# Expert biases as rows of a row group, loaded per block, with the first expert blocks and the record placing rearranged

## The chip, the cores and the metric

The kernel runs on one core of a Trainium2 chip. The metric is the device time in microseconds of one execution, as the median of repeated runs. The engines are PE (TensorE), DVE (VectorE), ACT (ScalarE), POOL (GpSimd) and SP (SyncE, which here only issues transfers).

## What is computed

A decoder block over 512 tokens of width 1024: a token mixer (gated short convolution and dilated attention), then a mixture of 32 experts, of which each token takes 4. The change touches the second part:

```python
logits = (hf @ w_router + b_router).astype(jnp.float32)
top_vals, top_idx = lax.top_k(logits, TOP_K)
gates = jax.nn.softmax(top_vals, axis=-1)
...
def expert_block(args):          # xb: 128 rows of one expert e
    xb, e = args
    gu = xb @ w_gate_up[e] + b_gate_up[e]
    gate, up = gu[:, :D_EXPERT], gu[:, D_EXPERT:]
    gate = jnp.minimum(gate, SWIGLU_LIMIT)
    up = jnp.clip(up, -SWIGLU_LIMIT, SWIGLU_LIMIT)
    act = (up + 1) * (gate * jax.nn.sigmoid(SWIGLU_ALPHA * gate))
    return act @ w_down[e] + b_down[e]
...
out = jax.ops.segment_sum(y_assign, sorted_tok, num_segments=T)
```

## The kernel before

Every engine's program is written out by hand in its own order; semaphores join them. The front (token mixer) streams 38 chunks of weights of 1 MiB. Its last stage is `wo`, which also gives the router's logits. Then comes **routing**: ranks of the tokens within their experts, the first rows for three experts found early, and `place_records`, which works out for each of the 2048 assignments a slot in a table in DRAM (`slot_dram`).

The **expert part** is a loop over blocks, here 32 (one per expert, 128 rows each). A block's weights are 12 chunks of 1 MiB: c = 0 to 7 are `w_gate_up` of this block's expert, c = 8 to 11 are `w_down` of the block before. For each chunk SP issues the load (`load_expert`, L526) into one of six raw buffers as soon as DVE has read that buffer's last content; ACT writes the upper part of the chunk in fp32r (`split_expert`, L1045), DVE the rest (L1351), into eight half-chunk units. PE multiplies with three products for each pair (`three`, L589): 16 units `gate_up` (L820), then 8 units `down` (L837) of the block before, 144 products of 512 columns in all. `used` counts the units that PE has finished, `split_lo` those that DVE has delivered.

Around these products PE also turns rows. `turn_act` (L805, after j = 1 and j = 3) turns the activations of the block before; `turn_rows` (L799, after k = 1 and k = 3 of `down`, by `next_rows`) the gathered rows of the next block. ACT and DVE copy each turned half out of PSUM (`turned`). POOL gathers rows from DRAM with an indirect transfer, and adds a block's result to `out` with another (`scatter`, with a read and write at the target). The column of indices for both it copies from `slots`, the table read back from DRAM. For blocks 0 to 2 the indices come from the early search instead; the gather of block 2's rows (`gather(4)`) stands on POOL behind the 16 transfers that write the records (L1606).

**Biases.** POOL cuts `b_gate_up` into three bf16 parts, stacked on 96 partitions (L1572 to L1577), and builds `sel`, a 96 x 128 selector for each block (L1579, for blocks past 32 L1641 in `over_step(4)`). In `gate_up` at k = 0 two products of `sel` with 512 columns set the bank (L828), so four a block. `b_down` is not added in the loop. In block 0 DVE makes a token-by-expert matrix of gates (`gates_by_expert`), PE turns it (L866) and multiplies it with `b_down` in fp32, four row groups of 32 for each half of the columns (`down_bias`, L858); ACT stores the result into `x2`, and POOL adds it to `out` by four indirect transfers (L1679) ahead of the loop of scatters.

Before block 0 PE runs `BUSY` = 14 products whose result nobody reads (L812).

## Time and profile before

| | us |
|---|---|
| median of 3 runs (lowest, highest) | 1700.66 (1699.68, 1701.02) |
| the profiled execution | 1699.82 |
| its span, from the first to the last instruction | 1697.8 |
| busy: PE, DVE, ACT, POOL | 1642.9, 1360.8, 1106.0, 330.3 |
| transferred | 484.45 MB, mean 285 GB/s |

The span is 2.0 us shorter than the execution's own time. Starts are given from the span's start. PE's records of successive products overlap (a product of 512 columns is recorded with 0.39 us), so pace is read from start to start, not from the length of a record.

### The profile page before, as it was taken

What the parts mean: (1) busy time and instruction counts of PE and PEld (TensorE: products, weight loads), DVE (VectorE), ACT (ScalarE), POOL (GpSimd) and SP (SyncE); (2) the same over time, 40 slices, a digit from 0 to 9 for tenths busy, and PEclk for the clock granted to TensorE, in tenths of its full rate; (3) what the DMA queues carried; (4) which work ended last, traced back from release to release, by engine and by line L of the source; (5) the groups of instructions that cost most, each with busy time, mean ns of one, the idle gap of its engine ahead of it and who ended that gap; (6) DMA issues with size and microseconds to landing.
All of it is one profiled execution on the core that took longest, in us unless ns stands there. A gap on an engine that the chain in (4) does not pass through costs nothing.

```text
span 1697.8 us, 23948 instructions
## 1 busy us (share of the span) xinstructions
PE 1642.9 (97%) x8021; PEld 1346.8 (79%) x8021; DVE 1360.8 (80%) x1124; ACT 1106.0 (65%) x1004; POOL 330.3 (19%) x176
## 2 busy tenths in 40 slices
PE   8999999999988899999999999999999999999995
PEld 5797777888886778877888888888888888888884
DVE  5974555533558889999999999999998999999994
ACT  5433433422345677877878878788777887777873
POOL 0000000500005523342222211222112211113210
PEclk9999999999998999999999999999999999999998
DMA  7331222332449999999999999999999999999993
GB/s 226 122 100 50 75 75 75 93 116 83 152 179 294 282 384 371 381 379 361 380 375 367 383 376 378 374 366 384 375 378 376 363 382 381 378 375 367 380 383 95
DMA packets 212404, 484.45 MB, mean 285 GB/s; under 512 B 12619, under 2 KB 55283, under 8 KB 195843
## 3 DMA queue, kind: packets, MB, share of 16 engines
q1 hardware_dynamic: 201168, 453.99, 72.4%
q0 software_dynamic: 11200, 29.96, 7.9%
q8 instruction: 25, 0.41, 0.1%
q14 instruction: 11, 0.09, 0.0%
HBM read 469.05 MB, written 23.77 MB: 290 GB/s over the span
## 4 chain that ended last, share of the span: by engine, by line
PE 53%; DVE 0%; issue 0%; ACT 0%; POOL 0%; ACTq 0%; DVEq 0%; POOLq 0%
PE ps L590 17%; PE ps L592 16%; PE ps L591 16%; PE ps L807 1%; PE ps L801 1%; PE ps L828 1%; DVE w_lo L1355 0%; ACT w_hi L1050 0%; POOL out L1667 0%; DVE oT L1512 0%; ACT r L1105 0%; DVE work L1502 0%; ACTq L213 0%; DVEq L1354 0%; ACTq L1049 0%
## 5 line engine op out<-in xcount | busy, mean ns | idle before, releaser
L1355 DVE TENSOR_TENSOR zT<-raw,zT 128x2048 fp32r<-128x2048 f32 x96 | 222.5, 2318 | 53.8 <-ACT zT L1050 51.1
L1355 DVE TENSOR_TENSOR w_lo<-more_raw,w_hi 128x2048 fp32r<-128x2048 f32 x96 | 217.3, 2289 | 24.1 <-ACT w_hi L1050 23.9
L1355 DVE TENSOR_TENSOR zT<-more_raw,zT 128x2048 fp32r<-128x2048 f32 x96 | 220.2, 2293 | 1.1 <-ACT zT L1050 1.1
L1355 DVE TENSOR_TENSOR w_lo<-raw,w_hi 128x2048 fp32r<-128x2048 f32 x96 | 216.7, 2284 | 1.2 <-issue 0.9
L590 PE MATMUL ps<-w_hi,xT 128*128 128x512 f32 x512 | 216.9, 424 | 0.0
L590 PE MATMUL ps<-zT,xT 128*128 128x512 f32 x512 | 203.0, 396 | 0.9 <-DVE zT L1355 0.7
L592 PE MATMUL ps<-w_hi,xT 128*128 128x512 f32 x512 | 201.2, 393 | 0.0
L591 PE MATMUL ps<-w_lo,xT 128*128 128x512 f32 x512 | 200.8, 392 | 0.0
L1050 ACT ACTIVATE zT<-more_raw 128x2048 fp32r<-128x2048 f32 x96 | 183.4, 1911 | 26.0 <-PE ps L592 21.6
L592 PE MATMUL ps<-zT,xT 128*128 128x512 f32 x512 | 199.7, 390 | 0.0
L1050 ACT ACTIVATE w_hi<-raw 128x2048 fp32r<-128x2048 f32 x96 | 183.4, 1910 | 24.8 <-PE ps L592 19.3
L591 PE MATMUL ps<-zT,xT 128*128 128x512 f32 x512 | 199.4, 389 | 0.0
L1667 POOL DMA_INDIRECT out<-r,uix x32 | 51.8, 1619 | 703.9 <-ACT r L1105 678.5
L1050 ACT ACTIVATE w_hi<-more_raw 128x2048 fp32r<-128x2048 f32 x96 | 180.0, 1908 | 5.7 <-DMA more_raw<-in_w_gate_up 5.7
L1050 ACT ACTIVATE zT<-raw 128x2048 fp32r<-128x2048 f32 x96 | 183.2, 1910 | 0.0
L1162 DVE TENSOR_TENSOR w_lo<-raw,w_hi 128x1024 fp32r<-128x1024 f32 x76 | 101.9, 1348 | 92.8 <-ACT w_hi L915 92.8
L590 PE MATMUL ps<-hT,w_hi 128*128 128x512 f32 x416 | 165.5, 398 | 2.6 <-DVE r L1323 1.6
L591 PE MATMUL ps<-hT,w_hi 128*128 128x512 f32 x416 | 162.5, 391 | 0.0
L592 PE MATMUL ps<-hT,w_lo 128*128 128x512 f32 x416 | 162.3, 390 | 0.0
L1588 POOL DMA_INDIRECT r<-expert_inputs,uix x33 | 94.9, 2874 | 199.8 <-DVE uix L1450 168.2
L915 ACT ACTIVATE w_hi<-raw 128x1024 fp32r<-128x1024 f32 x76 | 79.6, 1054 | 73.6 <-PE ps L592 68.0
L590 PEld LDWEIGHTS ps<-w_hi,xT 128*128 128x128 f32 x512 | 97.4, 190 | 25.4 <-issue 0.9
(257 smaller groups left out, 3378.3 us busy)
## 6 DMA issues: line engine op xcount, KB each, us to landing
more_raw<-in_w_gate_up SPq DMA_DIRECT2D x129, 1024.0 KB, 8.1
raw<-in_w_gate_up SPq DMA_DIRECT2D x127, 1024.0 KB, 7.7
raw<-in_w_down SPq DMA_DIRECT2D x65, 1024.0 KB, 8.1
more_raw<-in_w_down SPq DMA_DIRECT2D x63, 1024.0 KB, 7.6
raw<-in_w_in SPq DMA_DIRECT2D x29, 1024.0 KB, 5.4
r<-in_x SPq DMA_DIRECT2D x8, 512.0 KB, 5.8
raw<-in_w_branch_conv SPq DMA_DIRECT2D x4, 1024.0 KB, 5.0
raw<-in_w_out SPq DMA_DIRECT2D x4, 1024.0 KB, 4.9
```

The source lines that it names most:

```text
L590: pe.matmul(dst, a_hi, b_hi, start=start, stop=False)
L591: pe.matmul(dst, a_hi, b_lo, start=False, stop=False)
L592: return pe.matmul(dst, a_lo, b_hi, start=False, stop=stop)
L801: last = pe.transpose(ps[:, bk_T + half, P * k:P * k + P], xs[:, 4 * half + k::KD], ident)
L807: last = pe.transpose(ps[:, bk_T + half, P * k:P * k + P], act[:, half, k::4], ident)
L828: pe.matmul(ps[:, base + s, :], sel[:, bass.ds(g, 1), :], bpart[:, D * s + 512 * half:D * s + 512 * half + 512], start=True, stop=False)
L915: nc.scalar.activation(packed(w_hi, n), raw_unit(n, (n // 2) % RAW), ACT.Copy).then_inc(split_hi, 1)
L1050: nc.scalar.activation(expert_pair(0, c), chunk, ACT.Copy).then_inc(split_hi, 2)
L1162: nc.vector.tensor_tensor(packed(w_lo, n), raw_unit(n, (n // 2) % RAW), packed(w_hi, n).bitcast(F32), ALU.subtract).then_inc(split_lo, 1)
L1355: nc.vector.tensor_tensor(expert_pair(1, c), chunk, expert_pair(0, c).bitcast(F32), ALU.subtract).then_inc(split_lo, 2)
L1588: nc.gpsimd.indirect_dma_start(out=xs, out_offset=None, in_=h2_dram, in_offset=bass.IndirectOffsetOnAxis(ap=uix[:, col:col + 1], axis=0), ...
L1667: nc.gpsimd.indirect_dma_start(out=out, out_offset=bass.IndirectOffsetOnAxis(ap=uix[:, 1:2], axis=0), in_=ysb, in_offset=None, compute_op= ...
```

## The change

The biases of both matrices are cut into three bf16 parts by POOL during the front and kept in a DRAM tensor `bias_dram` as (expert, row of 512 columns, part). Per block SP loads six small pieces of 3 rows of 1 KB into partitions 0, 32, 64 and 96 of `brow`, between chunks 3 and 4. PE adds them with `ones_h` (3 rows x 128) as the other operand: four products for gate and up, each in its own row group and bank, and two for down, all after j = 3. `sel`, the selector products, `gates_by_expert`, its transposition, the fp32 products, `store_bias` and the four indirect additions are gone.

Both `turn_act` now follow j = 3, and both `next_rows` follow k = 3. A block begins when the first half of its rows is there. ACT and DVE copy both row halves after chunk 11. Block 0 turns the first half of block 1's rows after j = 11. Chunk 0 is split in the front, at `wo` 2. `place_records` is on POOL, 15 small operations after two lookups that stay on DVE. `BUSY` is 30 pairs of 192 and 96 columns. DVE's order follows ACT's. Line numbers of the changed file are some 20 to 30 higher.

```diff
-OVER_STEPS = 6
-BUSY = 14
+BUSY = 30
+NUP, NDOWN = 4, 2
+OVER_STEPS = 4
...
+                if CHUNKS[c] == ("wo", 0):
+                    sp.wait_ge(bias_parts_ok, 1)
+                    for part in range(3):
+                        sp.dma_start(braw[NE * part:NE * part + NE, 0:D], b_down[0]).then_inc(bias_in, 16)
...
+            def up_bias(e):
+
+                for r in range(NUP):
+                    sp.dma_start(brow[NE * r:NE * r + 3, 0:512], bias_dram[bass.ds(e, 1), r].rearrange(
+                        "o a n -> (o a) n")).then_inc(bias_rows_in, 16)
+
+            def down_bias(e):
+
+                for r in range(NDOWN):
+                    sp.dma_start(brow[NE * r:NE * r + 3, 512:1024], bias_dram[bass.ds(e, 1), NUP + r].rearrange(
+                        "o a n -> (o a) n")).then_inc(bias_rows_in, 16)
+
+            def load_block(g, e, earlier):
+
+                for c in range(CPE):
+                    if c == 4:
+                        sp.wait_ge(used, unit_base(g) - 11)
+                        up_bias(e)
+                        down_bias(earlier)
+                    load_expert(g, c, e if c < 8 else earlier)
+
...
+            sp.wait_ge(bias_kept, 16 * 6)
+            up_bias(0)
...
-            sp.wait_ge(h2T_pe, KD)
-            sp.wait_ge(h2_out, 16 * NB)
-            for b in range(NB):
-                sp.dma_start(bdn[NE * b:NE * b + NE, :], b_down[0]).then_inc(down_bias_in, 16)
...
-            for _ in range(BUSY):
-                pe.matmul(ps[:, bk_D, :], oT[:, 0, 0, 0:P], oT[:, 0, 1, :], start=True, stop=True)
+            for i in range(BUSY):
+                c = slice(P * (i % NB), P * (i % NB) + P)
+                pe.matmul(ps[:, bk_D, 0:192], oT[:, 0, 0, c], oT[:, 0, 1, 0:192], start=True, stop=True)
+                pe.matmul(ps[:, bk_D, 192:288], oT[:, 1, 0, c], oT[:, 0, 1, 0:96], start=True, stop=True)
...
-                if k == 0:
-                    for s in range(2):
-                        pe.matmul(ps[:, base + s, :], sel[:, bass.ds(g, 1), :],
-                                  bpart[:, D * s + 512 * half:D * s + 512 * half + 512],
-                                  start=True, stop=False)
...
+            def row_group(r):
+                return slice(NE * r, NE * r + 3)
+
+            def add_up_bias():
+
+                for r in range(NUP):
+                    s, half = divmod(r, 2)
+                    pe.matmul(ps[:, bk_A + 2 * half + s, :], ones_h[row_group(r), :], brow[row_group(r), 0:512],
+                              start=half == 1, stop=False)
+
+            def set_down_bias():
+
+                for r in range(NDOWN):
+                    pe.matmul(ps[:, bk_D + r, :], ones_h[row_group(r), :], brow[row_group(r), 512:1024],
+                              start=True, stop=False)
...
-            pe.wait_ge(turned_read, FIRST_ROWS)
-            def down_bias(n):
-
-                for b in range(NB):
-                    last = pe.matmul(ps[:, bk_D + b, :], gT[NE * b:NE * b + NE, :],
-                                     bdn[NE * b:NE * b + NE, 512 * n:512 * n + 512], start=True, stop=True)
-                last.then_inc(down_bias_pe, 1)
-
+            pe.wait_ge(turned_read, FIRST_ROWS - 1)
             for j in range(16):
+                if j == 4:
+                    pe.wait_ge(turned_read, FIRST_ROWS)
                 gate_up(0, j)
-                if j == 7:
-                    pe.wait_ge(gates_ok, 1)
-                    pe.transpose(ps[:, bk_D, 0:P], gmat.rearrange("p b e -> p (b e)"), ident).then_inc(gT_pe, 1)
-                if j == 10:
-                    pe.wait_ge(gT_ok, 1)
-                    pe.wait_ge(down_bias_in, 16 * NB)
-                    down_bias(0)
-                if j == 13:
-                    pe.wait_ge(bias_rows, 1)
-                    down_bias(1)
-            pe.wait_ge(bias_rows, 2)
-            next_rows(0, 0)
+                if j == 3:
+                    pe.wait_ge(bias_rows_in, 16 * NUP)
+                    add_up_bias()
+                if j == 11:
+                    next_rows(0, 0)
             next_rows(0, 1)
             with pe.Fori(1, nblk) as g:
-                pe.wait_ge(turned_read, tile(g, BEGIN))
+                pe.wait_ge(turned_read, tile(g, BEGIN) - 1)
                 for j in range(16):
-                    if j == 8:
-                        pe.wait_ge(act_ok, 2 * g + 1)
                     gate_up(g, j)
-                    if j == 1:
+                    if j == 3:
                         pe.wait_ge(act_ok, 2 * g)
                         turn_act(0)
-                    if j == 3:
                         pe.wait_ge(act_ok, 2 * g + 1)
+                        pe.wait_ge(turned_read, tile(g, BEGIN))
                         turn_act(1)
-                pe.wait_ge(y_ok, 2 * g)
+                        pe.wait_ge(bias_rows_in, 16 * (NUP + NDOWN) * g + 16 * NUP)
+                        add_up_bias()
+                        pe.wait_ge(y_ok, 2 * g)
+                        set_down_bias()
                 pe.wait_ge(turned_read, tile(g, ACT1))
                 for k in range(KD):
                     down(g, 16 + k, k)
-                    if k == 1:
+                    if k == 3:
                         next_rows(g, 0)
-                    if k == 3:
...
+                        if i == 2:
+                            sc.wait_ge(used, UF - 2)
+                            split_expert(0, 0)
...
-            for c in range(3):
-                split_expert(0, c)
-
+            split_expert(0, 1)
+            split_expert(0, 2)
             sc.wait_ge(top4_ok, 1)
             nc.scalar.activation(gate, gate, ACT.Exp).then_inc(gate_exp_ok, 1)
-            for c in range(3, XUN // 2):
-                split_expert(0, c)
+            split_expert(0, 3)
...
-            store_bias(0)
             split_expert(1, 0)
             split_expert(1, 1)
-            store_bias(1)
             turned(0, ROWS0, xTh[:, 0:4, :], bk_T)
+            split_expert(1, 2)
+            sigmoid(0, 1)
             turned(0, ROWS1, xTh[:, 4:8, :], bk_T + 1)
-            sigmoid(0, 1)
-            with sc.Fori(1, nblk) as g:
-                store_y(g, unit_base(g), g)
-                for c in range(2, CPE):
+            sc.sem_inc(y_ok, 2)
+
+            def turn_block(g, first):
+
+                for c in range(first, CPE):
                     split_expert(g, c)
-                    if c == 2:
+                    if c == 3:
                         turned(g, ACT0, aTh[:, 0:4, :], bk_T)
-                    if c == 3:
                         turned(g, ACT1, aTh[:, 4:8, :], bk_T + 1)
                     if c == 6:
                         sigmoid(g, 0)
                     if c == 10:
                         sigmoid(g, 1)
-                        turned(g, ROWS0, xTh[:, 0:4, :], bk_T)
+                turned(g, ROWS0, xTh[:, 0:4, :], bk_T)
                 turned(g, ROWS1, xTh[:, 4:8, :], bk_T + 1)
                 split_expert(g + 1, 0)
...
+            def block_offsets():
+
+                link(nc.vector.tensor_tensor(byoff.rearrange("p b k e -> p (b k) e"), oh,
+                                             off32.unsqueeze(1).to_broadcast([P, NREC, NE]), ALU.mult))
+                nc.vector.tensor_reduce(o16, byoff.rearrange("p b k e -> p (b k) e"), AX.X,
+                                        ALU.add).then_inc(lookups_ok, 1)
...
+            def bias_parts(n, rows, width):
+
+                hi, mid, wide = bpart[:, 0:width], btmp[:, 0:width], braw[:, 0:width]
+                gp.wait_ge(bias_in, 16 * 3 * (n + 1))
+                link(nc.gpsimd.tensor_copy(hi, wide))
+                link(nc.gpsimd.tensor_tensor(wide, wide, hi, ALU.subtract))
+                link(nc.gpsimd.tensor_copy(mid, wide))
+                link(nc.gpsimd.tensor_copy(hi[NE:2 * NE, :], mid[NE:2 * NE, :]))
+                link(nc.gpsimd.tensor_tensor(wide, wide, mid, ALU.subtract))
+                nc.gpsimd.tensor_copy(hi[2 * NE:3 * NE, :], wide[2 * NE:3 * NE, :]).then_inc(bias_parts_ok, 1)
+                gp.wait_ge(bias_parts_ok, n + 1)
+                for part in range(3):
+                    gp.dma_start(bias_dram[:, rows, part, :], hi[NE * part:NE * part + NE, :].rearrange(
+                        "e (r n) -> e r n", n=512)).then_inc(bias_kept, 16)
+                gp.wait_ge(bias_kept, 16 * 3 * (n + 1))
+
+            bias_parts(0, slice(0, NUP), 2 * D)
...
+            def place_records():
+
+                e16 = idxf
+                o16v = o16.rearrange("p (b k) -> p b k", b=NB)
+                over1, over2, over3 = [q16[:, i, :] for i in range(3)]
+                gp.wait_ge(lookups_ok, 2)
+                nc.gpsimd.tensor_scalar(over1, r16, P + 0.5, None, ALU.is_gt)
...
+                link(nc.gpsimd.tensor_tensor(o16, o16, over2, ALU.add))
+                nc.gpsimd.tensor_scalar(record_at[:, :], o16, -float(NCOL + 1), None, ALU.add).then_inc(places_ok, 1)
+                gp.wait_ge(places_ok, 1)
+
+            place_records()
...
-            gp.wait_ge(bias_rows, 2)
+            gp.wait_ge(slots_in, 16)
             gp.wait_ge(out_set, 16 * (NB + 1))
-            for b in range(NB):
-                nc.gpsimd.indirect_dma_start(
-                    out=out, out_offset=bass.IndirectOffsetOnAxis(ap=rec[:, TOPK * b, 0:1], axis=0),
-                    in_=x2[:, b, :], in_offset=None, compute_op=ALU.add).then_inc(out_biased, 16)
-            gp.wait_ge(slots_in, 16)
-            gp.wait_ge(out_biased, 16 * NB)
+
             def turn_round(before):
```

PE in a steady block, the operations from the last product of j = 2 on. Before (L590 to L592 are `three`, L807 is `turn_act`, L887 and L825 set up waits):

```order
L590 MATMUL ps<-w_hi,xT 128x512
L591 MATMUL ps<-w_lo,xT 128x512
L592 MATMUL ps<-w_hi,xT 128x512
L887 REGISTER_ALU
L807 MATMUL ps<-cst,work 128x128 x4
L825 REGISTER_ALU
L590 MATMUL ps<-zT,xT 128x512
```

With the change (L613 to L615 are `three`, L830 `turn_act`, L863 `add_up_bias`, L869 `set_down_bias`):

```order
L613 MATMUL ps<-w_hi,xT 128x512
L614 MATMUL ps<-w_lo,xT 128x512
L615 MATMUL ps<-w_hi,xT 128x512
L905 REGISTER_ALU
L830 MATMUL ps<-cst,work 128x128 x4
L907 REGISTER_ALU
L908 REGISTER_ALU
L830 MATMUL ps<-cst,work 128x128 x4
L910 ISA
L863 MATMUL ps<-r 128x512 x4
L869 MATMUL ps<-r 128x512 x2
L849 REGISTER_ALU
```

Both turns and all six bias products stand in one place; before, the turns stood in two, and the four bias products in two others.

POOL between the second gather and the third. Before (L1588 is `gather`, L1606 the record writes, L1612 the table's way back):

```order
L1588 DMA r<-expert_inputs,uix 128x1024
L1606 DMA slot_records<-rec,record_at 6144x2 x16
L1588 DMA r<-expert_inputs,uix 128x1024
L1612 DMA slots<-slot_records 128x96
```

With the change, the last eight of the 15 operations of `place_records` (L1609 to L1623) and what follows:

```order
L1616 TENSOR_TENSOR r<-r 128x16
L1617 TENSOR_TENSOR r<-r 128x16
L1618 TENSOR_SCALAR r<-r 128x16
L1619 TENSOR_TENSOR r<-r 128x16
L1620 TENSOR_TENSOR r<-r 128x16
L1621 TENSOR_TENSOR r<-r 128x16
L1622 TENSOR_TENSOR r<-r 128x16
L1623 TENSOR_SCALAR record_at<-r 128x16
L1630 DMA slot_records<-rec,record_at 6144x2 x16
L1589 DMA r<-expert_inputs,uix 128x1024
L1636 DMA slots<-slot_records 128x96
```

The third gather, of block 2's rows, now stands behind these operations too.

## Rows read from the trace of the kernel before

**Rows 1.** Timeline of PE, starts of blocks 0, 1, 2, 3, 6 and 31 (start, us).
```profile
522.95 0.61 PE L828 MATMUL ps<-r 96*128 96x512 bf16 x2 [1.56 <-DVE xT L1482]
...
555.40 0.60 PE L828 MATMUL ps<-r 96*128 96x512 bf16 x2 [1.76 <-DVE xT L1512]
...
595.16 0.89 PE L828 MATMUL ps<-r 96*128 96x512 bf16 x2 [4.03 <-DVE w_lo L1355]
...
634.12 0.60 PE L828 MATMUL ps<-r 96*128 96x512 bf16 x2
...
740.86 0.61 PE L828 MATMUL ps<-r 96*128 96x512 bf16 x2
...
1632.35 0.61 PE L828 MATMUL ps<-r 96*128 96x512 bf16 x2
```
**Rows 2.** Windows: span, busy PE, PEld, DVE, ACT, POOL; PEclk, DMA share, GB/s.
```profile
634.10:669.70 35.60, 35.60 (x166) 29.14 (x165) 33.64 (x23) 28.27 (x22) 10.27 (x5) 1.00 1.03 381
1240.97:1276.55 35.58, 35.58 (x166) 29.13 (x165) 33.06 (x23) 28.26 (x22) 7.04 (x4) 1.00 1.03 377
```
**Rows 3.** Timeline of ACT, two splits that waited for a transfer.
```profile
590.70 1.91 ACT L1050 ACTIVATE w_hi<-more_raw 128x2048 fp32r<-128x2048 f32 x1 [4.41 <-DMA more_raw<-in_w_gate_up]
...
653.80 1.92 ACT L1050 ACTIVATE w_hi<-raw 128x2048 fp32r<-128x2048 f32 x1 [0.57 <-DMA raw<-in_w_down]
```
**Rows 4.** Timeline of PE at the start of a steady block.
```profile
1240.74 0.39 PE L592 MATMUL ps<-zT,oT 128*128 128x512 f32 x1
1240.97 0.61 PE L828 MATMUL ps<-r 96*128 96x512 bf16 x2
...
1241.65 0.40 PE L591 MATMUL ps<-w_lo,xT 128*128 128x512 f32 x1
...
1243.92 0.39 PE L592 MATMUL ps<-w_hi,xT 128*128 128x512 f32 x1
1244.16 0.63 PE L807 MATMUL ps<-cst,work 128*128 128x128 f32 x4
...
1244.86 0.40 PE L591 MATMUL ps<-w_lo,xT 128*128 128x512 f32 x1
```
**Rows 5.** Timeline of PE around four fp32 products in four row groups.
```profile
542.97 0.39 PE L592 MATMUL ps<-w_hi,xT 128*128 128x512 f32 x1
543.28 1.14 PE L858 MATMUL ps<-r 32*128 32x512 f32 x8
...
544.69 0.40 PE L591 MATMUL ps<-w_lo,xT 128*128 128x512 f32 x1
```
**Rows 6.** Transfers, 300 to 330 us (front: rows of 1 KB): queue, packets, MB, share.
```profile
q1 hardware_dynamic: 3264, 3.93, 45.4%
```
**Rows 7.** Transfers, 570 to 590 us: all packets.
```profile
DMA packets 1702, 5.82 MB, mean 291 GB/s; under 512 B 129, under 2 KB 129, under 8 KB 1454
```
**Rows 8.** Timeline of PE, the products ahead of block 0.
```profile
514.26 6.24 PE L812 MATMUL ps<-oT 128*128 128x512 f32 x14
```
**Rows 9.** Timelines of DVE and POOL, from the placed records to the third gather.
```profile
530.90 0.17 DVE L1434 TENSOR_SCALAR record_at<-r 128x16 uint32<-128x16 f32 x1
...
562.68 2.57 POOL L1588 DMA_INDIRECT r<-expert_inputs,uix  x1 [0.30 <-PE ps L807]
```
**Rows 10.** Transfers, 562 to 563 us: the third gather, us to landing.
```profile
r<-expert_inputs,uix POOLq DMA_INDIRECT x1, 9.2
```
**Rows 11.** Timeline of POOL beside DVE's splits.
```profile
708.61 2.36 POOL L1654 COPY uix<-slots 128x1 uint32<-128x1 uint32 x1
...
717.24 7.80 POOL L1625 TENSOR_TENSOR work<-work 128x240 f32<-128x240 f32 x4 [2.36 <-DMA out<-r,uix]
725.12 0.22 POOL L1626 TENSOR_TENSOR r<-work 128x15 f32<-128x15 f32 x1
...
753.53 8.56 POOL L1641 TENSOR_SCALAR r<-r,cst 96x1920 bf16<-96x1920 f32 x1 [3.04 <-DMA out<-r,uix]
```
**Rows 12.** Timeline of DVE, the split beside the last of rows 11.
```profile
757.68 5.03 DVE L1355 TENSOR_TENSOR zT<-raw,zT 128x2048 fp32r<-128x2048 f32 x1
```

More of the change, by code:

```diff
@@ L572, in _ @@
                     before = sp.value_load(ublk[0:1, bass.ds(g - 1, 1)], min_val=0, max_val=NE - 1)
-                    for c in range(CPE):
-                        load_expert(g, c, e if c < 8 else before)
+                    load_block(g, e, before)
             last_e = sp.value_load(ublk[0:1, bass.ds(nblk - 1, 1)], min_val=0, max_val=NE - 1)
```

173 lines of the change are left out of this document (70 added, 103 removed).

## The prediction

> **What bounds the kernel now.** I read the windows first, then PE's timeline, then who waited for transfers. About 0.2% is what a measurement of this kernel can tell from no change.
>
> In a window of one steady block [rows 2] PE is busy for the whole 35.58 us at the full clock (PEclk 1.00), so PE sets the pace. The block starts [rows 1] say the same: 634.12 to 740.86 is three blocks of 35.58, and the 25 blocks from 740.86 to 1632.35 take 891.49, which is 25 x 35.58 plus 2.0 lost in one of them. The first blocks are dearer: block 0 takes 32.45 with only 16 of its 24 units, block 1 39.76, block 2 38.95.
>
> The same rows show a second limit right behind PE. The transfer engines' share is 1.03 in both windows, 377 GB/s in the steady one and 381 in the earlier one, where a split had to wait for its chunk [rows 2, 3]. A block moves what 377 GB/s carry in 35.58 us; at 381 it would take 35.2. I call this the **floor** of the transfers: 35.2 now, 0.4 below PE. A faster PE meets it almost at once, unless chunks lie ready.
>
> **Steady block, PE.** The pace of the products is (1243.92 - 1241.65) / 10 = 0.227 us [rows 4], and 144 of them make 32.69. From 1240.74 to 1241.65 are 0.91: two products (0.45) and the bias pair, 0.46. Two pairs a block cost 0.91, which go. From 1243.92 to 1244.86 are 0.94, so a turn of four costs 0.49, and its four transpositions 0.38 of that. 32.69 + 0.91 + 4 x 0.49 = 35.56, as measured.
>
> Now two turns stand together twice: 0.49 + 0.38 = 0.87 at best, 0.98 without any gain; I take 0.91, so 1.82 in all instead of 1.96. The six bias products are the open price. Four row groups at once are seen for the fp32 products: from 542.97 to 544.69 are 1.72 us, less two ordinary products 1.27 for eight records, which at 0.227 each one after another would be 1.81 at least [rows 5]. So they do run side by side. The lower end for up and down is two rounds at the pace of one product, 0.45; the upper is two rounds at 0.63, what an fp32 round took there, 1.27. Getting into that group took 0.31 where a product's pace is 0.23, so 0.08; I allow 0.2 for getting in and out, and take 0.65, nearer the lower end because fp32 records are also longer than others. The block is then 32.69 + 1.82 + 0.65 = **35.15** (34.9 to 35.8), 0.43 less.
>
> The Trainium skill (TensorEngine Tiling, Key Properties) says that a change of the tiling mode drains TensorE, which speaks against six small products in the middle of full-array ones. The 0.08 on the way in is the sign of it. If the way in and out cost 0.4 as an estimate from that rule, the block would be 35.35 and my sum 3.4 us higher.
>
> **Steady block, transfers.** Six pieces of 3 rows of 1 KB are added. In the front, where most packets have 1 KB, 3264 packets took 45.4% of 16 engines for 30 us, so 0.067 us each [rows 6]. Eighteen of them spread evenly over 16 engines add 0.08 us to a block; three rows can keep at most three engines busy, and if these are the same each time, each gets six packets, 0.40. A chunk has landed only when the slowest engine is done, so the floor becomes 35.3 to 35.6; I take 35.45. The issues stand on SP between chunks 3 and 4; the chunk behind them still has two others in flight, and I cost that at nothing; without such cover it would be the delay of one chunk in each block.
>
> What lies ready is used first. I take a lead of 5 us at block 2, about two chunks, from the freed time below; at 35.45 - 35.15 = 0.3 a block it lasts 17 blocks. So 17 x 0.43 + 14 x 0.13 = **9.1 us** saved (0 to 13.3).
>
> **Block 0.** 96 products are 21.8, biases 0.65, two turns 0.98: 23.4 instead of 32.45. What goes are 16 fp32 records, the turn of the gates, and the waits for DVE and ACT between them. Its chunks are split with the same spacing as before and its rows are turned at j = 11, some 5 us ahead of need. **-9.0** (-10 to -6).
>
> **Blocks 1, 2 and 6.** Block 2 waited 4.03 us for a split that had waited 4.41 for its transfer [rows 1, 3]. In the 20 us before, the engines moved only 291 GB/s [rows 7]: here lie the four additions of the bias to `out`. They are gone, so block 1 loses 4.2 above the steady 35.58 and block 2 3.4. Block 6 lost 2.0 when POOL built `sel` for 8.56 us and a DVE split beside it took 5.03 instead of 2.3 [rows 11, 12]; that operation is gone. Together **-9.6** (-9.6 to -4).
>
> **The start.** The 14 products ahead of block 0 take 6.24 [rows 8], 0.87 ns for each of 7168 columns, twice the steady 0.227 / 512, so PE is at its 1.2 GHz level there. The new ones have 8640 columns: 7.5 at that level, 1.3 more. PE then waited 1.56 for both halves of the rows [rows 1]; it now starts after the first, which I count as 0.6 earlier: **+0.7** (-0.5 to +3). The end gets its two down products within a wait: +0.2.
>
> **POOL.** This is what is late next. `place_records` ended at 531.07 on DVE, the third gather started at 562.68 and landed 9.2 later, at 571.9 [rows 9, 10]: 40.8 us from placed records to block 2's rows. With block 0 starting at 523.6 and block 1 at 547.0, PE turns these rows after k = 3 of block 1, 20 units and the additions or 28.8 us on, at 575.8. So the records must be placed by 535.0. I expect DVE's lookups to end about 528, as they stand behind one split more and lack the small operations; that leaves 7 us for 15 operations. Such an operation costs 0.22 when free, but one with DVE splitting beside it 2.36, and four in a row 7.80, 1.95 each [rows 11]. In block 0 a split of 2.3 comes each 2.7 us, so some gaps are left; I take 0.75 each, 11.2 us, and a stall of PE of **+4.2** (0 to +22). What covered such a delay before is that the rows landed some 10 us ahead of their turn; without cover every microsecond on POOL counts in full.
>
> **Sum.** 0.7 - 9.0 - 9.6 - 9.1 + 4.2 + 0.2 = -22.6. The profiled execution took 1699.82 (span 1697.8), so 1677.2; the median of the runs is 0.84 higher, which gives **1678**.
>
> **The rivals.** (1) *Neither transfers nor POOL bind.* The steady blocks give 13.3 and the stall is 0: -31.0, 1669.7. For it: the share of 1.03 is nearly the same when no split waits. Against: 377 and 381 GB/s lie close.
>
> (2) *The three engines carry all small rows.* Floor 35.6, so after 11 blocks nothing is gained: 4.7 instead of 9.1, and 1682.5. The Trainium skill (DMA: Bandwidth & Descriptors, on the number of engines of one transfer) says that a transfer from SP uses the largest number up to 16 that divides its slowest dimension, and the lowest-numbered ones, which for three rows are the same three; no view here shows single engines.
>
> (3) *POOL is held by DVE.* At 1.3 us an operation they take 19.5 and PE stalls 12.5: 1686.4; at 1.95 it stalls 22 and the gain is only 5. For it: four in a row did take 1.95 each. Against: that was with DVE splitting without a gap.
>
> (4) *Slower: small transfers hold the queue.* If each of the six costs all engines a fixed time, as a chunk's end might, the floor rises by six times that. Without the stall the rest of the change is worth 0.7 - 9.0 - 9.6 + 0.2 = -17.7. The sum turns positive when the floor passes 36.15 in all 31 blocks, that is at 0.16 us for each small transfer. At 0.3 the floor is 37.0: 31 x 1.42 = 44 less 17.7, slower by 26, 1727. For it: the share of 1.03 says that the engines have no free time now. Against: a packet of 1 KB cost only 0.067 us [rows 6].
>
> **Chances.** Forecast 0.40; (1) 0.18; (2) 0.15; (3) 0.15; (4) 0.07; terms that cancel to within 0.2% of no change 0.05. Faster is 0.88. The range from 1667 to 1691 takes in (1), (2), most of (3) and the bounds of start and bias products; it leaves out the worst of (3), (4) and no change.
>
> **What would show it.** Right: steady blocks of 35.15, then near 35.4, with splits that begin to wait for chunks in the later ones; six bias records in about 0.65; block 0 near 23.4; blocks 1 and 2 without a wait for a chunk; a wait of PE ahead of the row turn in block 1. Wrong: steady blocks at 35.58 or above from the start (floor), six records one after another over 1.3 us, or record writes on POOL starting before 534 or after 550.

## The result and the profile after

| | median of runs, us | lowest, highest |
|---|---|---|
| before (5 runs) | 1700.01 | 1698.0, 1701.02 |
| with the change (5 runs) | 1707.19 | 1706.09, 1710.1 |

The ratio worked out from all fast runs is 1.0052, 95% interval 1.0041 to 1.0063 (the two medians alone divide to 1.0042): slower by half a per cent, where 1678 was forecast. The profiled execution took 1710.1 us, the longest of the five; its span is 1708.3.

The page of the changed kernel, section 1 and two groups of ACT's splits from section 5. The splits of the expert part stand at L948 (ACT) and L1232 (DVE) now, where they were at L1050 and L1355: these lines lie lower in the changed file, not higher.

```profile
PE 1654.0 (97%) x8114; PEld 1349.9 (79%) x8114; DVE 1349.1 (79%) x1097; ACT 1100.4 (64%) x1001; POOL 278.6 (16%) x197
...
L948 ACT ACTIVATE zT<-more_raw 128x2048 fp32r<-128x2048 f32 x96 | 183.7, 1913 | 60.7 <-DMA more_raw<-in_w_gate_up 40.1
...
L948 ACT ACTIVATE w_hi<-raw 128x2048 fp32r<-128x2048 f32 x96 | 184.1, 1918 | 41.4 <-DMA raw<-in_w_down 28.8
```

POOL is less busy than before (330.3), as intended. The splits now stand idle 40.1 and 28.8 us for transfers. Before, the largest wait for transfers in a group of the expert part's splits was 5.7.

PE's timeline, starts of blocks 0, 1, 2, 3, 6, 7 and 31, to be laid beside [rows 1]:

```profile
531.04 0.79 PE L613 MATMUL ps<-w_hi,xT 128*128 128x512 f32 x1 [0.56 <-DVE xT L1476]
...
556.79 0.48 PE L613 MATMUL ps<-w_hi,xT 128*128 128x512 f32 x1
...
592.18 0.39 PE L613 MATMUL ps<-w_hi,xT 128*128 128x512 f32 x1
...
627.46 0.40 PE L613 MATMUL ps<-w_hi,xT 128*128 128x512 f32 x1
...
733.29 0.40 PE L613 MATMUL ps<-w_hi,xT 128*128 128x512 f32 x1
...
769.07 0.50 PE L613 MATMUL ps<-w_hi,xT 128*128 128x512 f32 x1
...
1640.04 0.50 PE L613 MATMUL ps<-w_hi,xT 128*128 128x512 f32 x1
```

Three things stand here. Block 0 starts 7.8 us later than before (531.04 against 523.21, its first product of 512 columns there). Blocks 1 to 5 are short: 35.39, then 35.28 each, 105.83 for the three from 627.46. From block 6 on they are long: the 24 blocks from 769.07 to 1640.04 take 870.97, 36.29 each, 0.7 more than the 35.58 of before.

ACT's timeline in block 19 shows what the long blocks wait for:

```profile
1215.16 1.92 ACT L948 ACTIVATE zT<-more_raw 128x2048 fp32r<-128x2048 f32 x1 [1.36 <-DMA more_raw<-in_w_gate_up]
...
1219.04 1.92 ACT L948 ACTIVATE zT<-raw 128x2048 fp32r<-128x2048 f32 x1 [0.63 <-DMA raw<-in_w_gate_up]
1221.60 1.92 ACT L948 ACTIVATE w_hi<-raw 128x2048 fp32r<-128x2048 f32 x1 [0.64 <-DMA raw<-in_w_down]
1224.10 1.92 ACT L948 ACTIVATE w_hi<-raw 128x2048 fp32r<-128x2048 f32 x1 [0.57 <-DMA raw<-in_w_down]
1226.59 1.92 ACT L948 ACTIVATE zT<-more_raw 128x2048 fp32r<-128x2048 f32 x1 [0.57 <-DMA more_raw<-in_w_down]
```

Five splits in a row start only when their chunk lands: the transfers set the pace. (The chunk of the first of them landed at 1215.00.) Yet the window of block 20, with the same columns as [rows 2], shows fewer GB/s than before (369 for 377) and no higher share of the engines (1.02 for 1.03):

```profile
1239.08:1275.35 36.27, 35.85 (x167) 28.91 (x166) 32.95 (x23) 28.28 (x22) 5.85 (x4) 1.00 1.02 369
```

So the mean over 16 transfer engines does not show the limit. The landings do. Each of the 16 engines raises a chunk's semaphore when its share is in. From those times, over the 17 blocks between 1000 and 1600 us, comes this table: for chunk c, the time from the last landing of the chunk ahead to its own last landing; their sum; and how far the last engine is behind the middle one, at c0 (at c6 and c7 it is more, up to 7.5 in the change). Where a landing is missing from the record, the others are used, so a sum is good to about 0.02. "PE" means that PE paces the transfers there. The other kernels follow below (no_small is no_small_loads, sixteen is sixteen_rows, bef_small is before_small_loads).

```
              c0   c1   c2   c3   c4   c5   c6   c7   c8   c9  c10  c11   sum  behind
before      2.71 2.71 2.71 2.71 2.68 2.68 2.71 3.71 4.76 3.19 2.48 2.52 35.58 PE 0.7
the change  2.69 2.69 2.91 2.76 3.08 2.67 5.74 3.77 2.50 2.49 2.54 2.53 36.36    4.6
no_small    2.71 2.70 2.71 2.70 2.66 2.68 5.42 3.93 2.49 2.49 2.51 2.52 35.53    3.7
two_copies  2.71 2.70 2.76 2.77 2.70 2.67 5.40 3.95 2.49 2.49 2.51 2.52 35.67    3.9
sixteen     2.71 2.70 2.88 2.63 3.07 2.68 5.12 3.96 2.49 2.49 2.51 2.51 35.76    3.8
spare_three 2.71 2.69 2.69 2.79 3.08 2.67 5.30 3.96 2.49 2.49 2.52 2.52 35.92    4.1
bef_small   2.71 2.70 2.71 2.71 3.09 2.68 5.17 3.95 2.50 2.49 2.52 2.51 35.74    4.0
late_issue  2.71 2.71 2.70 2.67 2.70 2.69 2.69 5.19 3.63 2.59 2.49 2.53 35.31 PE 1.8
```

A chunk of `w_gate_up` lands 2.7 us behind the one ahead, one of `w_down` 2.5; the gather and the scatter come in around c6 to c9. In the kernel before all 16 engines finish a chunk within some 1.5 us. With the change one is 4.6 us behind the middle, and a chunk has landed only when that one is done. It is a single engine: the next to last is 3.6 us ahead of it (median over these chunks), in no_small_loads 0.4, where five or so are late together.

### The profile page after: what moved, and what is told of

Read it like the earlier page. It is cut to its first block and busy times, and to the rows that moved or that the text cites. A ratio compares the mean times of both kernels' runs of the same rounds, so it can differ in the third digit from the quotient of the medians.

```text
span 1708.3 us, 24726 instructions
## 1 busy us (share of the span) xinstructions
PE 1654.0 (97%) x8114; PEld 1349.9 (79%) x8114; DVE 1349.1 (79%) x1097; ACT 1100.4 (64%) x1001; POOL 278.6 (16%) x197
## 5 line engine op out<-in xcount | busy, mean ns | idle before, releaser
L1232 DVE TENSOR_TENSOR zT<-raw,zT 128x2048 fp32r<-128x2048 f32 x96 | 217.4, 2291 | 57.9 <-ACT zT L948 56.8
L1232 DVE TENSOR_TENSOR zT<-more_raw,zT 128x2048 fp32r<-128x2048 f32 x96 | 221.0, 2302 | 21.4 <-ACT zT L948 21.0
L1232 DVE TENSOR_TENSOR w_lo<-more_raw,w_hi 128x2048 fp32r<-128x2048 f32 x96 | 216.9, 2286 | 10.0 <-ACT w_hi L948 9.7
L948 ACT ACTIVATE zT<-more_raw 128x2048 fp32r<-128x2048 f32 x96 | 183.7, 1913 | 60.7 <-DMA more_raw<-in_w_gate_up 40.1
L1232 DVE TENSOR_TENSOR w_lo<-raw,w_hi 128x2048 fp32r<-128x2048 f32 x96 | 216.7, 2284 | 3.2 <-ACT w_hi L948 3.2
L948 ACT ACTIVATE w_hi<-raw 128x2048 fp32r<-128x2048 f32 x96 | 184.1, 1918 | 41.4 <-DMA raw<-in_w_down 28.8
L613 PE MATMUL ps<-w_hi,xT 128*128 128x512 f32 x512 | 203.4, 397 | 0.6 <-DVE xT L1476 0.6
L613 PE MATMUL ps<-zT,xT 128*128 128x512 f32 x512 | 203.3, 397 | 0.0
L615 PE MATMUL ps<-w_hi,xT 128*128 128x512 f32 x512 | 200.5, 392 | 0.0
L615 PE MATMUL ps<-zT,xT 128*128 128x512 f32 x512 | 199.6, 390 | 0.0
L948 ACT ACTIVATE zT<-raw 128x2048 fp32r<-128x2048 f32 x96 | 180.4, 1915 | 13.5 <-DMA raw<-in_w_gate_up 13.4
L948 ACT ACTIVATE w_hi<-more_raw 128x2048 fp32r<-128x2048 f32 x96 | 180.7, 1918 | 7.3 <-issue 7.3
L1186 DVE TENSOR_TENSOR w_lo<-raw,w_hi 128x1024 fp32r<-128x1024 f32 x76 | 95.3, 1261 | 95.3 <-ACT w_hi L940 95.3
L613 PE MATMUL ps<-hT,w_hi 128*128 128x512 f32 x416 | 166.0, 399 | 2.6 <-DVE r L1356 1.6
L615 PE MATMUL ps<-hT,w_lo 128*128 128x512 f32 x416 | 162.5, 391 | 0.0
L613 PEld LDWEIGHTS ps<-zT,xT 128*128 128x128 f32 x512 | 96.0, 188 | 33.7 <-issue 13.4
L613 PEld LDWEIGHTS ps<-w_hi,xT 128*128 128x128 f32 x512 | 96.7, 189 | 30.8 <-DVE w_lo L1232 10.2
```

Source lines behind the costliest of these rows:

```text
L613: pe.matmul(dst, a_hi, b_hi, start=start, stop=False)
L615: return pe.matmul(dst, a_lo, b_hi, start=False, stop=stop)
L948: nc.scalar.activation(expert_pair(0, c), chunk, ACT.Copy).then_inc(split_hi, 2)
L1186: nc.vector.tensor_tensor(packed(w_lo, n), raw_unit(n, (n // 2) % RAW), packed(w_hi, n).bitcast(F32), ALU.subtract).then_inc(split_lo, 1)
L1232: nc.vector.tensor_tensor(expert_pair(1, c), chunk, expert_pair(0, c).bitcast(F32), ALU.subtract).then_inc(split_lo, 2)
```

## The experiments

Each was run beside the kernel before on the same chip, whose median lay between 1698.6 and 1699.8; the ratios are to that. Blocks of 35.27 are those that PE paces. Four of the kernels (no_small_loads, sixteen_rows, spare_three and late_issue) leave out the biases of all experts but expert 0, and so serve only to time the parts.

### The start: busy14

```diff
-BUSY = 30
+BUSY = 14
-            for i in range(BUSY):
-                c = slice(P * (i % NB), P * (i % NB) + P)
-                pe.matmul(ps[:, bk_D, 0:192], oT[:, 0, 0, c], oT[:, 0, 1, 0:192], start=True, stop=True)
-                pe.matmul(ps[:, bk_D, 192:288], oT[:, 1, 0, c], oT[:, 0, 1, 0:96], start=True, stop=True)
+            for _ in range(BUSY):
+                pe.matmul(ps[:, bk_D, :], oT[:, 0, 0, 0:P], oT[:, 0, 1, :], start=True, stop=True)
```

> The changed kernel with the 14 products of 512 columns back in place of the 30 pairs of 192 and 96 columns. Theory (the pairs take 12.8 us at the 1.2 GHz level and do not lift the clock, so block 0's first 12 products run at that level too): the loop takes 6.1 us, 6.7 less, the turns and the first 12 products are 0.8 and 2.4 us shorter, and everything behind is shifted as a whole: 1707.2 - 9.5 = 1697.7 (1696 to 1700). Rival (the transfers are the bound from block 1 on, whenever PE starts, so an earlier start only makes PE wait for chunks sooner): under 3 us gained, 1704 to 1707.

Measured: 1700.01, ratio 1.0004 (0.9995 to 1.0013). 7.2 gained of 9.5: the shift passes through to the end, so the rival falls. What was lost on the way stands in block 1. First the start, in PE's timeline of the changed kernel:

```profile
515.69 0.53 PE L836 MATMUL ps<-oT 128*128 128x192 f32 x1
516.01 0.34 PE L837 MATMUL ps<-oT 128*128 128x96 f32 x1
516.15 0.49 PE L836 MATMUL ps<-oT 128*128 128x192 f32 x1
516.44 0.34 PE L837 MATMUL ps<-oT 128*128 128x96 f32 x1
...
528.52 1.96 PE L824 MATMUL ps<-cst,r 128*128 128x128 f32 x8
531.04 0.79 PE L613 MATMUL ps<-w_hi,xT 128*128 128x512 f32 x1 [0.56 <-DVE xT L1476]
...
535.04 0.63 PE L613 MATMUL ps<-w_hi,xT 128*128 128x512 f32 x1
535.47 0.63 PE L614 MATMUL ps<-w_lo,xT 128*128 128x512 f32 x1
...
536.31 0.39 PE L613 MATMUL ps<-w_hi,xT 128*128 128x512 f32 x1
536.54 0.40 PE L614 MATMUL ps<-w_lo,xT 128*128 128x512 f32 x1
```

Thirty pairs last 12.83 us, from 515.69 to 528.52. The next product starts 0.29 behind one of 192 columns and 0.14 behind one of 96, which looks like a price by the column. The weight loads, of which each product has one of its own, say otherwise (PEld, same kernel):

```profile
520.12 0.33 PEld L837 LDWEIGHTS ps<-oT 128*128 128x128 f32 x1
520.33 0.33 PEld L836 LDWEIGHTS ps<-oT 128*128 128x128 f32 x1
520.54 0.33 PEld L837 LDWEIGHTS ps<-oT 128*128 128x128 f32 x1
520.76 0.33 PEld L836 LDWEIGHTS ps<-oT 128*128 128x128 f32 x1
```

They start 0.213 apart, whichever product follows, and PEld is busy without a gap from 515.69 to 528.50. The eight transpositions of 128 columns behind the pairs are 0.213 apart too (529.21, 529.42, 529.64). So at the level of 1.2 GHz a product cost 0.213 us with 96, 128 and 192 columns alike, and 60 of them are 12.8. A product of 512 columns took 0.43 there. That it is the load which sets the 0.213 fits the full PEld row; no run sets it apart from another fixed cost of a product. The 1.48 ns a column, by which before_pairs below is forecast, is only the quotient of this mix. The Trainium skill (TensorE: Matmul & The Clock Gate, Back-to-back issue gap) says that in a stream of weight loads and products both set the spacing, so that a formula by columns comes out too low for small products. The trace agrees.

Nor do the pairs lift the clock: the granted clock stays at 1.2 GHz, the products of block 0 follow at 0.43 until 536.31, then at 0.23. With 14 products of 512 columns it had risen 6 us after the first of them, before block 0.

Then block 1. PE and POOL of busy14:

```profile
522.72 0.50 PE L613 MATMUL ps<-w_hi,xT 128*128 128x512 f32 x1 [0.96 <-DVE xT L1474]
...
577.51 1.16 PE L824 MATMUL ps<-cst,r 128*128 128x128 f32 x8 [2.28 <-DMA r<-expert_inputs,uix]
...
578.79 0.63 PE L614 MATMUL ps<-zT,oT 128*128 128x512 f32 x1
579.22 0.63 PE L615 MATMUL ps<-zT,oT 128*128 128x512 f32 x1
...
582.16 0.39 PE L613 MATMUL ps<-zT,oT 128*128 128x512 f32 x1
```

```profile
526.89 0.29 POOL L1607 TENSOR_SCALAR r<-r 128x16 f32<-128x16 f32 x1 [3.79 <-DVE r L1433]
...
528.28 2.29 POOL L1613 TENSOR_SCALAR r<-r 128x16 f32<-128x16 f32 x1
530.66 2.32 POOL L1614 TENSOR_TENSOR r<-r 128x16 f32<-128x16 f32 x1
...
536.65 0.26 POOL L1621 TENSOR_SCALAR record_at<-r 128x16 uint32<-128x16 f32 x1
...
569.47 1.98 POOL L1587 DMA_INDIRECT r<-expert_inputs,uix  x1 [0.31 <-issue]
```

Here is the stall that was forecast. The 15 operations take 10.0 us, from 526.89 on, three of them held for 2.2 to 2.3 us by a split; the third gather starts at 569.47, and PE waits 2.28 for its rows. Behind this short wait the granted clock is 1.2 GHz from 578.68 to 582.09, and the nine products from 578.43 to 582.16 take 3.73 instead of 2.04: 1.7 more. Block 1 takes 39.57 instead of 35.39: 4.2, of which these two are 4.0. In the change itself DVE's lookups and POOL's operations came 8.6 us later too, but the operations took only 5.8 (535.46 to 541.3), and the later block 1 hid the gather: its stall is nought only because PE was late.

### The steady blocks: no_small_loads

```diff
-                    if c == 4:
-                        sp.wait_ge(used, unit_base(g) - 11)
-                        up_bias(e)
-                        down_bias(earlier)
```

> The changed kernel without the six small bias transfers of each block from block 1 on; leaves out the loading of the biases past expert 0, so every block adds expert 0's. Theory (the small transfers raise the time the transfer engines need for a block from about 35.45 to 36.2 us and more): PE's block of 35.28 holds until the lead is used up, then blocks of 35.45; 25 blocks by 36.3 - 35.4 = 0.9 are 22 us, so 1685 (1682 to 1688). Rival (the blocks are longer because of the new order of the gather, the scatter and the splits, not because of the copies): blocks stay near 36.2 and the time is over 1703.

Measured: 1686.35, ratio 0.9926 (0.9914 to 0.9938), as the theory said. Blocks 3 to 15 take 35.29 on average, blocks 16 to 30 35.54 (the change: 35.94 and 36.35). The six small transfers are worth 21 us; without them the change would be faster than the kernel before. The transfers' own limit is 35.53, by the table.

### two_copies

```diff
-                for r in range(NUP):
-                    sp.dma_start(brow[NE * r:NE * r + 3, 0:512], ...
+                sp.dma_start(brow[0:P:8, 0:512], bias_dram[bass.ds(e, 1), 0:NUP].rearrange(
+                    "o r a n -> (o r a) n")).then_inc(bias_rows_in, 16)
-                for r in range(NDOWN):
-                    sp.dma_start(brow[NE * r:NE * r + 3, 512:1024], ...
+                sp.dma_start(brow[0:P // 2:8, 512:1024], bias_dram[bass.ds(e, 1), NUP:NUP + NDOWN].rearrange(
+                    "o r a n -> (o r a) n")).then_inc(bias_rows_in, 16)
-                return slice(NE * r, NE * r + 3)
+                return slice(NE * r, NE * r + 17)
```

A fourth, unused row fills up each group in `bias_dram`, and POOL sets `brow` to zero once.

> The changed kernel with two bias transfers per block instead of six: one of 16 rows of 1 KB (a fourth, unused row in each group) and one of 8 rows, on partitions 0, 8, 16, ...; PE reads 17 rows of a group, those between being zero. If three transfer engines carry all small rows at 0.19 us each (six rows on each of three engines), the rows are now spread, one or two on each engine, and a block needs 0.2 to 0.4 us more than without them instead of 0.75 to 0.9: 1707.2 - 25 x 0.5 = 1695 (1691 to 1699). If the cost is a fixed one for each transfer, a third is left: 1707.2 - 25 x 0.6 = 1692. If it is one for each row or byte in all, more rows cost more: 1709 to 1715.

Measured: 1690.9, ratio 0.995 (0.9937 to 0.9962). A block needs 0.14 more than without bias transfers, less than either account said, with 24 rows instead of 18. That more rows cost more is refuted; between a price per transfer and one per engine this run does not decide.

### sixteen_rows

```diff
-                        up_bias(e)
-                        down_bias(earlier)
+                        for r in range(6):
+                            sp.dma_start(spare_rows[0:16, 48 * r:48 * r + 48], b_gate_up[0][r:r + 1, 0:768].rearrange("o (a n) -> (o a) n", a=16)).then_inc(spare_in, 16)
```

> As no_small_loads (the biases past expert 0 left out), with six unused transfers per block in place of the bias transfers, each of 16 rows of 192 bytes, the same 18 KB in all. Theory (what counts is the number of small rows on the transfer engine that lands last, whatever their size): every engine now carries six small rows, so the last one too, and the block costs as much as with 3-row transfers: 36.2 to 36.4 in the second half, 1702 to 1708. Rival A (bytes count): less than one microsecond in all, 1687. Rival B (the three rows happen to lie on the engines that are last anyway, and six rows on all engines cost only their own 0.4): 35.9, 1695.

Measured: 1693.79, ratio 0.9965 (0.9951 to 0.9978): nearest to rival B. 96 rows of 192 bytes in six transfers cost 0.23 a block, chunk 4 alone 0.4, of which 0.3 come back at c6. The 18 KB are the same as in the change, so it is not the bytes that set the price, and a row of 192 bytes lands 0.19 us behind the one ahead on the same engine, as a row of 1 KB does. Against that, the change's six cost 0.83. So "it is the number of rows on the last engine" falls as the whole account.

### before_small_loads

```diff
+            def small_copies():
+                for r in range(6):
+                    sp.dma_start(spare_rows[0:3, 256 * r:256 * r + 256], b_gate_up[0][r:r + 1, 0:768].rearrange(
+                        "o (a n) -> (o a) n", a=3)).then_inc(small_in, 16)
...
+                    if c == 4:
+                        small_copies()
                     load_expert(g, c, g if c < 8 else g - 1)
```

> The kernel before with six unused transfers of 3 rows of 1 KB per block, issued between chunks 3 and 4, from block 1 to 31. Theory: blocks of the transfer engines 35.45 + 0.75 to 0.9 = 36.2 to 36.35, above PE's 35.58, once the lead of some 6 us is used up (block 14 or so): 15 blocks by 0.7 give 10 us, 1710 (1706 to 1716). Rival (small transfers cost only their bytes, 0.08 us a block, and the changed kernel lost its time elsewhere): no change, 1700.

Measured: 1702.33, ratio 1.0018 (1.001 to 1.0027). The sign is right, the size a third: blocks are longer only from the sixteenth on, 35.76 instead of 35.58. The table has chunk 4 at 3.09, as dear as in the change, but c2, c3 and c6 are not.

### spare_three

The six transfers of before_small_loads, put into no_small_loads, behind the change's wait of 11 units (SP issues them right behind chunk 3 in the change, so this wait holds nothing up there).

> As no_small_loads (the biases past expert 0 left out), with six unused transfers per block of 3 rows of 1 KB in place of the bias transfers, into partitions 96 to 98 and from an input, as in before_small_loads. There the transfers of a block took 35.74, here 36.36 with the change's own six. Theory (the frame decides: order of gather, scatter and waits of the changed kernel): blocks of 36.2 to 36.4 in the second half, 1703 to 1708. Rival (where the rows come from and go to decides, partitions 0 to 98 of a table in DRAM against 96 to 98): 35.53 + 0.4 = 35.9, 1694 to 1698.

Measured: 1698.42, ratio 0.9997 (0.9988 to 1.0006): the rival, by its block length. The same six transfers cost 0.39 here as well (35.92 against 35.53), nearly all at chunk 4. The change's own, of the same shape, cost 0.83. At chunk 4 both cost the same (3.08); the other 0.44 a block stand mostly at c2 and c6 of the change's row. What is left to differ is where the rows come from or go to (`bias_dram` and partitions 0 to 98, against an input and partitions 96 to 98), since PE never waits for them between 700 and 1600 us; this is argued from the difference, and which of the two it is wasn't tried apart. two_copies has the change's source and spreads its rows over partitions 0 to 120, and cost only 0.14.

The landings of the change's six transfers of block 19 show how they run (issued from 1193.69 to 1196.71, us):

```
1194.94 1195.39 1195.82 1196.26 1196.71 1197.14                 one for each, at the issue
1200.21 1200.40 1200.58 1200.78 1200.97 1201.16                 an engine
1200.65 1200.84 1201.03 1201.22 1201.41 1201.60                 a second
1204.04 1204.24 1204.44 1204.64 1204.84 1205.02                 a third, right behind chunk 3 (1203.85)
```

Three engines carry one row of each transfer, 0.19 us apart. Their first rows land 0.2 us behind the three last landings of chunk 3 (1200.01, 1200.44 and 1203.85), so they appear to be the three engines that were last with chunk 3. By a rule of the Trainium skill (DMA: Bandwidth & Descriptors, Why a DMA increments its semaphore by 16 and not by 1) a transfer of three rows uses three engines, and the issuer counts the other 13 at once; the trace agrees, with three late landings and one early for each. The Trainium skill's advice to coalesce small transfers (same page, Rules for kernel authors) is worth 16 us here, 1707.2 against 1690.9. How much of it is due to fewer transfers and how much to more engines is not shown; six transfers on all engines (sixteen_rows) cost 0.23 a block, two cost 0.14.

### late_issue

```diff
                     if c == 4:
-                        sp.wait_ge(used, unit_base(g) - 11)
-                        up_bias(e)
-                        down_bias(earlier)
+                        sp.wait_ge(used, unit_base(g) - 4)
+                        for r in range(1):
+                            sp.dma_start(spare_rows[0:1, 0:16], b_gate_up[0][r:r + 1, 0:16]).then_inc(spare_in, 16)
```

> The changed kernel without the six bias transfers past block 0 (leaves out the biases of the experts past 0, as no_small_loads), but SP waits ahead of chunk 4 until PE has four units of the block before left, and issues one transfer of one row of 64 bytes there: chunk 4 is issued about as late behind chunk 3 as with six copies. Rival to be tested (the six copies cost because SP needs 3.5 us for them and chunk 4 comes late): blocks near 36.3 in the second half, 1703 or more. Theory (the queue still holds three chunks then, so a late issue costs nothing): as no_small_loads, 1686 to 1688.

Measured: 1681.99, ratio 0.9894 (0.9879 to 0.9909). SP's issue time is not the cause. More than that, and forecast by neither account: this is 4.4 us faster than no_small_loads. All blocks stay at 35.27, and the last engine is 1.8 us behind instead of 3.7. Holding chunk 4 back lowers the floor below PE's time.

### change_held and before_pairs

The first moves only that wait in the changed kernel, from 11 to 4 units. The second puts the 30 pairs into the kernel before.

> The changed kernel with that one wait moved from 11 units to 4, its six transfers per block as they are. Theory: the floor falls by the 0.2 to 0.3 us that the wait was worth in late_issue, but six rows on the last engine still cost over 0.4: blocks of 35.9 to 36.1 in the second half, 1700 (1697 to 1703). Rival (the depth of the queue was the whole cause): blocks of 35.3, 1683 to 1687. Rival (SP is then late with chunk 4 by 3.5 us more, and this is too late): 1707 or above.

> The kernel before with the 30 pairs of 192 and 96 columns in place of its 14 products of 512 columns. Theory (a product costs 1.48 ns a column there whatever the number of columns, and the clock stays at 1.2 GHz until some 5 us into block 0): block 0 starts 6.7 us later plus 0.8 for the turns, its first 12 products cost 2.4 more: 1699.5 + 9.5 = 1709 (1706 to 1710). Rival (block 0 of the kernel before waits for DVE and ACT anyway, and a later start gives them the time): 1702 to 1705.

Measured: change_held 1698.57, ratio 0.9997 (0.9988 to 1.0006); steady blocks of 35.92 instead of 36.35. So one constant is worth 8.6 us, as forecast, and makes up for the loss. before_pairs 1706.81, ratio 1.0047 (1.0033 to 1.006): 8.1 us slower than the kernel before beside it. Block 0 starts at 530.95, 7.7 us late as with the change, and is itself only 1.8 shorter, so the waits in the old block 0 hide little of it, as the theory said.

### best, best_no_busy and best_held

two_copies with 14 products, and the gather of block 2's rows earlier:

```diff
             for n in range(NREC):
                 nc.gpsimd.indirect_dma_start(
                     out=slot_dram, ...
-            gp.wait_ge(turned_pe, tile(1, BEGIN))
-            gather(4)
+                if n == 5:
+                    gp.wait_ge(turned_pe, tile(1, BEGIN))
+                    gather(4)
```

> two_copies, with BUSY as 14 products of 512 columns, and the gather of block 2's rows moved on POOL to behind the sixth record write (before: behind the sixteenth). Theory: two_copies less 8.3 for the start and 2.4 for block 0's clock as in busy14, and without the 4.2 that PE lost there in block 1 to the late gather: 1690.9 - 10.5 = 1680.4 (1678 to 1684). If the transfers, not PE, set the time from block 1 on, less is gained: 1686 to 1690.

> best without any of the products ahead of block 0. In busy14 the rows for block 0 had landed some 4 us before these products ended. Theory: block 0 starts 4 us earlier but at the 1.2 GHz level, 12 products at 0.43 instead of 0.227 us cost 2.4 us: 1.5 us faster than best, 1679. Rival: the clock stays at the lower level for longer, since the turns and their waits stand between, or block 1's rows come late: no gain or up to 3 us slower.

> best with SP's wait ahead of the bias transfers and chunk 4 later: until PE has 4 units of the block before left, not 11. In late_issue this wait kept all blocks at 35.27 and the last engine 1.8 us behind the middle one instead of 3.7. Theory (a queue filled less deeply when the gather and the scatter come keeps the transfer engines together): all steady blocks of best at 35.3 to 35.4 instead of 35.3 to 36.0, 6 us less: 1675 (1673 to 1678). Rival (late_issue was faster only because it had no bias rows at all, and two_copies' rows cost their 0.14 us a block in any order): 1680.

Measured: best 1680.61, ratio 0.9882 (0.9867 to 0.9898); best_no_busy 1682.12, 0.9899 (0.9883 to 0.9914); best_held 1674.41, 0.9853 (0.9838 to 0.9868), the fastest of all and 1.5% faster than the kernel before. In best block 1 takes 35.39, so the stall of busy14 is gone. Without the 14 products block 0 starts only 2.2 us earlier, at 521.12, and is 1.8 longer, so the 1.5 us forecast for leaving them out did not come. The granted clock rose at 524.93 there, 3.8 us into block 0; behind the thirty pairs it took 5.3. In best_held PE waits for nothing between 700 and 1600 us, where in the change it waits for DVE's splits:

```profile
PE ps L613 <- DVE w_lo L1232: 8.7, 21, 0.6
```

(us in all, times, the longest; the view books only part of the 1.0 us a block that the change loses there). Its blocks 3 to 15 take 35.27 on average and 16 to 30 35.34; in best they take 35.29 and 35.67.

## Why the prediction was wrong

Where the 10.5 us between the two spans (1697.8 and 1708.3) come from, beside the terms forecast:

| part | forecast | measured |
|---|---|---|
| start, to block 0's first product of 512 columns | +0.7 | +7.8 |
| block 0 (32.45 to 25.75) | -9.0 | -6.7 |
| blocks 1, 2 and 6, with their share of the steady gain | -10.9 | -9.8 |
| the other 27 blocks up to 30 | -7.7 | +16.2 |
| POOL's operations | +4.2 | 0 |
| block 31 and the end | +0.1 | +3.1 |

**The steps that held.** The steady block of PE: 35.15 forecast, 35.28 measured. The double turn and the bias products, in the changed kernel's steady block:

```profile
1244.42 0.39 PE L615 MATMUL ps<-w_hi,xT 128*128 128x512 f32 x1
1244.65 1.11 PE L830 MATMUL ps<-cst,work 128*128 128x128 f32 x8
1245.70 0.40 PE L863 MATMUL ps<-r 3*128 3x512 bf16 x4
1245.92 0.38 PE L869 MATMUL ps<-r 3*128 3x512 bf16 x2
1246.23 0.50 PE L613 MATMUL ps<-zT,xT 128*128 128x512 f32 x1
1246.57 0.39 PE L614 MATMUL ps<-zT,xT 128*128 128x512 f32 x1
```

1246.57 - 1244.42 less two products is 1.70, where 0.91 + 0.65 = 1.56 were forecast: the six products run in two rounds, as said, and the groups together are 0.14 dearer. Blocks 1, 2 and 6 lost their extra time as forecast (4.2 and 3.4 in blocks 1 and 2). Block 0 is 23.31 in busy14, where 23.4 was forecast; in the change its first twelve products at the lower clock add the 2.4 missing. POOL's term comes out at 4.2 in busy14, but by luck: 2.3 are wait and 1.7 clock, where all of it was forecast as wait.

**First failed step: the floor of the transfers.** "35.2 now", "I take 35.45", against 36.36: 24 of the 33 us between the two sums. It has two parts. The base was taken from the GB/s of two windows; it is 35.53, and that stood in the trace of before: the slack between a chunk's landing and its split, at the start of a block, grew from 3.0 us in block 3 to 3.6, 3.8 and 3.9, while splits further on waited for chunks. A lead that grows by only 0.1 to 0.2 a block of 35.58 means a floor of about 35.4. Then the small transfers: 0.08 to 0.40 was the range, 0.83 was measured, of which 0.39 is what six such spare ones cost too and 0.44 is the change's own. At 1.1 a block instead of 0.3 the lead was used up after block 5, not after 17 blocks. The term put at nothing, chunk 4 issued late behind the six, was rightly put so: late_issue shows a gain by it. Rival (2), three engines that carry all small rows, had the picture right and the price too low: it took the busy time of a packet, 0.067, where rows land 0.19 apart (six such steps, 1.1, are more than a block lost, so this is not its price either). Rival (4), slower by small transfers, had its point of decision at 36.15, and its outcome came true at 36.36 with a chance of 0.07. Its mechanism, a fixed time on all engines for each transfer, is not what happened: six transfers of sixteen rows cost less than six of three. That its sum for 36.36, 31 x 0.78 - 17.7 = +6.5, comes near is luck: only 24 blocks were long, and the start brought the rest.

**Second failed step: the start.** "7.5 at that level, 1.3 more" took ns a column from products of 512 columns. What counts is the number of products: 60 at 0.213 are 12.8, whatever their columns. [rows 4] had the warning: four transpositions of 128 columns took 0.38, so 0.095 each at the full clock, where 128 columns at the pace of a product of 512 would be 0.057. At half the clock, 60 of them come to 11.4. The bounds of +3 were too near. That the clock would not rise was no term at all. Of the 0.6 for starting after the first half of the rows 0.35 were gained (2.52 from the loop's end to the first product, 2.87 before). The rest, 1.4, was lost ahead of the loop: it starts at 515.69, not at 514.26.

Each of the two steps is worth about the whole loss: busy14, without the second, and change_held, with a lower floor, both measure the same as the kernel before (1.0004 and 0.9997).

**The stall on POOL** was in the sum at 4.2 and came out at nought, since the late start covered it.

**What stays open.** Why one transfer engine falls behind the others (in the change a single one, without the small transfers several), and why holding chunk 4 back by some 4 us keeps them together: both are seen in the landings (3.7 against 1.8), neither is explained. Nor is it known whether the source or the target of the bias rows costs the 0.44. In block 31 the time from its start to the last product lay between 49.3 and 51.7 in all kernels, without an order.

## What to carry to other kernels

Where transfers run without a gap, measure their limit from the landings of successive chunks, last engine by last engine, not from the GB/s of a window; a mean over 16 engines hides the one that counts. Against such a limit a few KB in several narrow transfers cost as much as hundreds of KB: put them into one with many rows, and try when it is issued, since one constant in a wait was worth 8.6 us. Cost a product from a row of its own size: with few columns and weights of its own for each, count products, not columns. If it is there to raise the clock, look whether it does.

## What was not expected of the hardware

- These small products did not lift the clock: 12.8 us of pairs of 192 and 96 columns left it at 1.2 GHz, while after 6 us of products of 512 columns it stood at 2.4.
- Products of 96, 128 and 192 columns, each with its own weight load, all cost 0.213 us at 1.2 GHz.
- Behind a wait of PE of 2.28 us the clock was back at 1.2 GHz for nine products, 1.7 us more.
- A chunk issued later made the transfers faster: 1681.99 against 1686.35 in kernels that differ, besides that wait, only by one transfer of 64 bytes a block.
- Rows of 192 bytes and of 1 KB in small transfers land at the same spacing, 0.19 us, on one engine.
